# A hybrid SSD and HGRN2 trunk: dt block behind C, first convolution tap on ScalarE, states ahead of the taps, four output blocks begun together

## The reference

```python
h = rmsnorm(x, mix_norm[l])
z, xbc, dt_raw, q_raw, f_raw, i_raw, g_raw = split(h @ w_in[l])
xbc = silu(causal_depthwise_conv(xbc, conv_w, conv_b))      # 4 taps, B, C and xs
dt  = softplus(dt_raw + dt_bias);  a_cum = cumsum(dt * A)   # 8 heads
y_ssd = rmsnorm_groups((intra + inter + d * xs) * silu(z))  # SSD, state carried over chunks
f = lb + (1 - lb) * sigmoid(f_raw);  logf = log(f)          # HGRN2 gate
b = cumsum of logf over 16-token chunks
o = intra(q*exp(b-b_ref), k*exp(b_ref-b)) + inter(q*exp(b), state)
y_hg = rmsnorm_heads(o) * silu(g_raw)
x = x + concat(y_ssd, y_hg) @ w_out[l]
x = x + 0.5 * swiglu(rmsnorm(x))
```

## Time and profile before

| | us |
|---|---|
| median of three runs | 2044.61 (2044.28 to 2046.07) |
| profiled execution | 2046.51 |
| its span | 2044.7 |
| TensorE busy | 1989.8 (97% of the span) |
| VectorE busy | 801.9 (39%) |
| ScalarE busy | 661.9 (32%) |
| GpSimd busy | 845.4 (41%) |
| mean granted TensorE clock | 0.983 of full |

### The profile page before, as it was taken

The page is one execution under the profiler, slowest core; times in us unless marked ns, Lnnn a source line. Parts: engine busy times, 40 slices in busy tenths (PEclk is TensorE's granted clock), DMA queues, the critical chain, the costliest instruction groups (busy, mean ns, idle before and its releaser), DMA issues.

```text
span 2044.7 us, 29020 instructions
## 1 busy us (share of the span) xinstructions
PE 1989.8 (97%) x10636; PEld 1636.5 (80%) x10636; DVE 801.9 (39%) x1268; ACT 661.9 (32%) x903; POOL 845.4 (41%) x362
## 2 busy tenths in 40 slices
PE   7999999989989999999999999999799999999998
PEld 6888888867777888888888888888677778888887
DVE  7322211497786222221142222117778752222112
ACT  4323223343343322322232322224333332323222
POOL 3544444432223344444444444444322234444453
PEclk9999999989999999999999999999899899999999
DMA  3322333212112222233322223322211123223332
GB/s 136 122 92 94 97 94 95 93 63 69 58 52 87 85 96 97 98 94 94 101 94 94 100 94 95 96 89 82 73 64 52 43 92 101 94 92 100 96 94 91
DMA packets 55813, 181.62 MB, mean 89 GB/s; under 512 B 8369, under 2 KB 10417, under 8 KB 55729
## 3 DMA queue, kind: packets, MB, share of 16 engines
q1 hardware_dynamic: 55728, 180.52, 27.6%
HBM read 178.40 MB, written 2.10 MB: 88 GB/s over the span
## 4 chain that ended last, share of the span: by engine, by line
PE 84%; DVE 10%; issue 3%; ACT 1%; DMA 0%; DVEq 0%; SPq 0%; ACTq 0%
PE ps L1253 27%; PE ps L1254 27%; PE ps L1255 27%; DVE acc L865 1%; PE ps L1426 1%; DVE xs L904 1%; ACT th L510 1%; DVE b L872 1%; DVE lm L1058 1%; DVE g L852 0%; PE ps L1475 0%; DVE b L868 0%; PE ps L1268 0%; DVE e L939 0%; PE ps L1488 0%
## 5 line engine op out<-in xcount | busy, mean ns | idle before, releaser
L437 POOL TENSOR_TENSOR wlo<-raw,whi 128x1024 fp32r<-128x1024 f32 x348 | 843.1, 2424 | 1188.4 <-ACT whi L470 621.7
L1253 PE MATMUL ps<-hhi,whi 128*128 128x512 f32 x1776 | 703.0, 396 | 14.4 <-DVE w L967 13.7
L1254 PE MATMUL ps<-hlo,whi 128*128 128x512 f32 x1776 | 697.1, 393 | 0.0
L1255 PE MATMUL ps<-hhi,wlo 128*128 128x512 f32 x1776 | 696.6, 392 | 0.0
L1253 PEld LDWEIGHTS ps<-hhi,whi 128*128 128x128 f32 x1776 | 337.1, 190 | 91.3 <-issue 21.7
L1255 PEld LDWEIGHTS ps<-hhi,wlo 128*128 128x128 f32 x1776 | 337.0, 190 | 71.1
L1254 PEld LDWEIGHTS ps<-hlo,whi 128*128 128x128 f32 x1776 | 337.2, 190 | 68.6
L470 ACT ACTIVATE whi<-raw 128x1024 fp32r<-128x1024 f32 x168 | 177.2, 1056 | 344.6 <-PE ps L1255 344.6
L1255 PE MATMUL ps<-ahi,wlo 128*128 128x512 f32 x704 | 273.9, 389 | 0.0
L1253 PE MATMUL ps<-ahi,whi 128*128 128x512 f32 x704 | 273.9, 389 | 0.0
L1254 PE MATMUL ps<-alo,whi 128*128 128x512 f32 x704 | 273.9, 389 | 0.0
(11 more groups left out here) (228 smaller groups left out, 1466.1 us busy)
## 6 DMA issues: line engine op xcount, KB each, us to landing
raw<-in_up SPq DMA_DIRECT2D x168, 512.0 KB, 3.2
raw<-in_mix SPq DMA_DIRECT2D x66, 512.0 KB, 3.3
raw<-in_dn SPq DMA_DIRECT2D x64, 448.0 KB, 3.3
raw<-in_dn SPq DMA_DIRECT2D x32, 512.0 KB, 3.5
raw<-in_lead SPq DMA_DIRECT2D x12, 512.0 KB, 3.3
stage<-in_x SPq DMA_DIRECT2D x4, 512.0 KB, 7.0
out<-stage SPq DMA_DIRECT2D x8, 256.0 KB, 2.7
raw<-in_mix SPq DMA_DIRECT2D x4, 256.0 KB, 2.5
```

What stands on the lines that cost most here:

```text
L437: pool.tensor_tensor(wlo[:, q, :], raw[:, q, :], whi[:, q, :].bitcast(F32), ALU.subtract).then_inc(split.sem, 1)
L1253: mm(dst, whi[:, q, s], mh, start=start, stop=False)
L1254: mm(dst, whi[:, q, s], ml, start=False, stop=False)
L1255: return mm(dst, wlo[:, q, s], mh, start=False, stop=stop)
```

## The change

- `PROJ`: f3 and q0 move up and the dt block goes behind C; the value blocks follow q0 as before.
- The gate: `gate_f` is cut in two, the reciprocal goes straight into `b`, and the affine `b` operation on VectorE is replaced by scale and bias of ScalarE's Ln. Scans and the first distances stand before q0's bank is read; `hg_q(0)` and `query_levels(0)` come before `hg_dist(1)` and `hg_k(1)`.
- dt: `dt_first` behind C's work, `dt_rest` in the step of q3, `dt_turn` behind g0, `chunk_ends` behind xs0; TensorE waits for `dt_sum` and `b_tok` before the last k tile of g0.
- Convolution: the first tap, with its bias, is a ScalarE activation (`conv_start`); `hg_dist` stands ahead of the other taps of B and C, `ssd_states` ahead of those of xs1 to xs3.
- Output projection: blocks 0 to 3 each do their `SOON` tiles in four banks (4, 5, 0, 2), with `group_sums(1)` behind block 0's and `group_spreads(1)` behind block 2's, then their `LATE` tiles; the rest as before. On VectorE the last gates and norms change places.

The diff, without unchanged lines and step counts:

```diff
-PROJ = ([("f", 0), ("f", 1), ("f", 2), ("dt", 0), ("f", 3)]
-        + [("q", 0), ("q", 1), ("B", 0), ("q", 2), ("C", 0), ("q", 3), ("g", 0)]
+PROJ = ([("f", 0), ("f", 1), ("f", 2), ("f", 3), ("q", 0)]
+        + [("q", 1), ("B", 0), ("q", 2), ("C", 0), ("dt", 0), ("q", 3), ("g", 0)]
...
-VALUES_AFTER = 5
+VALUES_AFTER = 4
...
     if n < 0:
-        return VALUES_AFTER + k0 // 2
+        return VALUES_AFTER + 1 + k0 // 2
...
+        MIXED = (4, 5, 0, 2)
...
+                def conv_start(t, n):
+                    i = {"B": CONV_B, "C": CONV_C}.get(t, t)
+                    ready(proj_out, n)
+                    do(conv_first, conv_src(t), xr[:, 0:T], ACT.Identity,
+                       scale=par[:, CW + 4 * i:CW + 4 * i + 1], bias=par[:, CB + i:CB + i + 1])
...
+                def gate_log(p):
+                    ready(f_gate, p)
+                    do(f_log, b[:, p, :], b[:, p, :], ACT.Ln, scale=par[:, OLB + p:OLB + p + 1],
+                       bias=par[:, LB + p:LB + p + 1])
...
-                    if kind == "dt":
-                        ready(dt_abs)
-                        do(dt_exp, acb[:], acb[:], ACT.Exp)
...
                         for p in range(NP - 1):
-                            ready(f_gate, p)
-                            do(f_log, b[:, p, :], b[:, p, :], ACT.Ln)
-                        ready(dt_exp)
-                        do(dt_log, acb[:], acb[:], ACT.Ln, bias=1.0)
+                            gate_log(p)
                     if n == VALUES_AFTER:
-                        ready(f_gate, NP - 1)
-                        do(f_log, b[:, NP - 1, :], b[:, NP - 1, :], ACT.Ln)
+                        gate_log(NP - 1)
...
-                        hi(VALUES0 + 1 + NS)
-                        hg_exps(1)
...
-                        hi(VALUES0 + 2 + NS)
-                        hi(VALUES0 + 3 + NS)
+                        for i in range(1, VALUES):
+                            hi(VALUES0 + i + NS)
...
+                        hg_exps(1)
...
+                    if kind in ("B", "C"):
+                        conv_start(kind, n)
...
-                        ready(to_end)
-                        do(to_end_exp, wend[:], wend[:], ACT.Exp)
...
+                    if kind == "dt":
+                        ready(dt_abs)
+                        do(dt_exp, acb[:], acb[:], ACT.Exp)
+                        ready(dt_exp)
+                        do(dt_log, acb[:], acb[:], ACT.Ln, bias=1.0)
...
+                    if n == AT["z", 0]:
+                        ready(to_end)
+                        do(to_end_exp, wend[:], wend[:], ACT.Exp)
                     if kind == "xs":
+                        conv_start(pr, n)
...
+                            ssd_sq(3)
...
-                        if pr == 2:
-                            ssd_sq(3)
...
-                def gate_f(p):
+                def gate_first(p):
...
-                    did(dve.reciprocal(acc[:], t1[:]))
+                    did(dve.reciprocal(b[:, p, :], t1[:]))
+                def gate_last(p):
...
-                    did(stt(km[:, p, :], km[:, p, :], BIG, acc[:], ALU.min, ALU.mult))
-                    made(f_gate, ts(b[:, p, :], acc[:], col(OLB + p), col(LB + p), ALU.mult, ALU.add))
+                    made(f_gate, stt(km[:, p, :], km[:, p, :], BIG, b[:, p, :], ALU.min, ALU.mult))
...
-                def convolve(t, n):
+                def convolve(t):
...
-                    ready(proj_out, n)
-                    did(ts(dst, xr[:, 0:T], col(CW + 4 * i), col(CB + i), ALU.mult, ALU.add))
+                    ready(conv_first, CONVS.index(t))
                     for k in range(1, 4):
-                        settle()
+                        if k > 1:
+                            settle()
...
                 for n, (kind, pr) in enumerate(PROJ):
-                    evac(n)
-                    if n in (1, 2):
-                        gate_f(n - 1)
-                    if kind == "dt":
-                        dt_first()
-                        gate_f(2)
+                    if n != AT["q", 0]:
+                        evac(n)
+                    if kind == "f":
+                        if pr:
+                            gate_last(pr - 1)
+                        gate_first(pr)
                     if n == AT["f", 3]:
-                        gate_f(3)
-                        for p in range(NP - 1):
+                        gate_last(3)
+                    if n == AT["q", 0]:
+                        scan_f(0)
+                        hg_dist(0)
+                        for p in range(1, NP):
...
-                        hg_dist(0)
-                        scan_f(NP - 1)
-                        dt_rest()
+                        evac(n)
...
-                        hg_dist(1)
-                        did(dve.tensor_copy(acbs[0:8, :], acb[:]))
-                        settle()
-                        made(acb_split, tt(acbs[32:40, :], acb[:], acbs[0:8, :].bitcast(F32), ALU.subtract))
-                        hg_k(1)
-                    if n == AT["q", 0]:
...
+                        hg_dist(1)
+                        hg_k(1)
...
-                        if pr == 1:
-                            dt_out()
-                        if pr == 2:
-                            end_weights()
+                        if pr == 3:
+                            dt_rest()
...
+                        if pr == 3:
+                            ready(dt_sum)
+                            settle()
+                            did(dve.tensor_copy(acbs[0:8, :], acb[:]))
+                            settle()
+                            made(acb_split, tt(acbs[32:40, :], acb[:], acbs[0:8, :].bitcast(F32), ALU.subtract))
                     if kind in ("B", "C"):
-                        if kind == "B":
-                            ends()
-                        convolve(kind, n)
...
+                        convolve(kind)
...
+                    if kind == "dt":
+                        dt_first()
...
+                        dt_out()
...
-                        convolve(pr, n)
-                        conv_out(pr)
+                            ends()
...
+                        convolve(pr)
+                        conv_out(pr)
...
+                        else:
+                            end_weights()
...
-                    if kind == "g" and pr in (1, 2):
+                    if n == AT["g", 1]:
+                        ssd_states(3)
...
-                        silu(("g", pr), g2[:, 0, :], gs[:, pr % 2, :])
-                        if pr == 1:
-                            ssd_states(3)
-                        hg_gate(pr)
-                        if pr == 1:
-                            ssd_norm(0)
-                            ssd_norm(1)
-                            hg_norm(2, 3)
-                            hg_norm(3, 4)
-                            hg_lo(1)
-                        else:
-                            ssd_lo(0)
-                            ssd_lo(1)
-                            hg_lo(2)
-                            ssd_gate(3)
-                group_rsqrt(1)
+                        silu(("g", 1), g2[:, 0, :], gs[:, 1, :])
+                        hg_gate(1)
+                        ssd_norm(0)
+                        ssd_norm(1)
+                        hg_norm(2, 3)
+                        hg_norm(3, 4)
+                        hg_lo(1)
+                    if n == AT["g", 2]:
+                        ready(proj_out, n)
+                        silu(("g", 2), g2[:, 0, :], gs[:, 0, :])
+                        ssd_lo(0)
+                        ssd_lo(1)
+                        ssd_gate(3)
+                        hg_gate(2)
+                        hg_lo(2)
...
+                group_rsqrt(1)
+                hg_lo(3)
...
-                hg_lo(3)
...
-                        return stt(x[:, m, :], bank(DOWN + m % 2), 1.0, x[:, m, :], ALU.mult, ALU.add)
+                        return stt(x[:, m, :], bank(MIXED[m % 4]), 1.0, x[:, m, :], ALU.mult, ALU.add)
...
                 def b_turn():
-                    ready(to_end)
...
-                        ready(dt_sum)
...
-                        ready(b_tok)
+                        ready(to_end)
...
+                        if k == KD - 1 and n == AT["g", 0]:
+                            ready(b_tok)
+                            ready(dt_sum)
...
-                    if n == AT["q", 1]:
-                        dt_turn()
-                    if n == AT["B", 0]:
-                        chunk_ends()
...
                     if n == AT["g", 0]:
+                        dt_turn()
...
+                    if n == AT["xs", 0]:
+                        chunk_ends()
...
                                   else (ohi[:, k - NP, :], olo[k - NP][:]))
-                        last = products(bank(DOWN + m % 2), w % NS, k, moving, k == SOON[0], k == LATE[-1])
+                        last = products(bank(MIXED[m % 4]), w % NS, k, moving, k == SOON[0], k == LATE[-1])
...
```

(19 more changed lines are left out.)

## The result

The changed kernel takes 2024.98 us (median of four runs, 2022.80 to 2028.35) against 2044.44 us of the kernel before in the same rounds: ratio 0.9902, 95% interval 0.9881 to 0.9923. It is faster by 19.5 us; forecast were 40.8 us and 2004 us, with a range to 2021. The profiled execution took 2024.67 us, its span is 2022.9 us, the granted clock 0.990.

A forecast was written before the change was run, and what follows sets the result against it. TensorE, busy 97% of the span, was taken as the bound, with its idle and half-clock time to win. Gains 32.6 + 6.0 + 14.2 = 52.8 less new waits 12.0 gave net 40.8 us: 2044.61 to 2004 us, range 1990 to 2021.

The forecast's parts named there:

- Head of the mixer: End of the values to first HGRN2 outputs: `w` and `ks` waits with slow clock cost 16.3 us; 1.5 us remains.
- This wait goes: Head of the mixer: `ks` would be ready at 430.5 to 432.7 against TensorE's 432.6, so its wait disappears.
- B to g0: Mixer stretch that receives the moved dt chain: new waits of together 2.0 us per layer.
- The `dt_sum` term: At g0's last k, TensorE would newly wait 1.3 us for `dt_sum`, bounds 0 and 3.
- it is not on TensorE's path unless tanh of q3 is late, and that is hidden behind a GpSimd hold: Beside q3: two more ScalarE table switches per layer, 1.28 us each, would not delay TensorE.
- By the page's figure tanh of q3 would be 2.7 us later: At q3: with a switch costing 2.66 us, 2 us more over both layers, left out of the sum.
- SSD pairs: In the SSD pairs: states moved ahead of the taps remove four `st` waits, gaining 6.0 us.
- Output projection: Last projection matmul to FFN norm sums: `sqb` wait and slow clock, 7.1 us per layer, go; 2.5 new waits come.
- take VectorE some 2.8 each ... hidden: Output projection: four first residuals in a burst take VectorE 2.8 us each, hidden behind blocks 4 to 7 of 5.44.
- Waits of up to 1.8 us did not lower it: Argument against the upper-ends rival: TensorE waits of up to 1.8 us had not lowered the clock.
- waits at their upper ends: Rival for the whole mixer: new waits reach 20 us or more per layer, about 2018 to 2035; chance 0.20.
- The rival of GpSimd's hold: Rival, f0 to g0: 17 subtractions hold VectorE, which becomes the mixer's bound; slower, 2046 to 2055 us; chance 0.04.

The follow-up runs named there:

- e5: Changed kernel with GpSimd subtracting only 8 of 1024 columns per weight block after the first four, so VectorE is not held (result wrong): 1989.48 us.
- e6: Kernel before the change with GpSimd subtracting only 8 of 1024 columns per weight block after the first four (result wrong): 1990.6 us.
- e15: Changed kernel with e5's cut of GpSimd's subtraction and e1's order on ScalarE (result wrong): 1986.87 us.
- e1: Changed kernel with ScalarE's dt Exp and Ln placed behind the tanh of q3 instead of ahead of it: 2015.13 us.
- e12: Changed kernel with dt's Ln replaced by a second Exp, two table loads fewer per layer (result wrong): 2022.97 us.
- e7: Changed kernel with the dt block one place earlier, between q2 and C, and `dt_rest` in C's step: 2022.12 us.
- e2: Changed kernel with e1's order, and TensorE waiting for `dt_sum` only behind g0's outputs, right before the turn: 2020.74 us.
- e14: Changed kernel with the SSD states put back behind the convolution's taps: 2035.29 us.
- e8: Kernel before the change with only the output projection's part of the change: 2039.76 us.
- e13: Changed kernel with the first convolution tap and its bias back on VectorE: 2027.62 us.
- e11: Changed kernel with each GpSimd subtraction cut into four operations of 256 columns, plus e1's order: 2000.49 us, the fastest version that computes all.
- e3: Changed kernel with the 32 narrow head-sum matmuls cut in four groups of eight between xs1's k tiles: 2036.55 us.

## Why the prediction was wrong

The direction was right, and so were three of the four waits and the stages at both ends of the mixer taken whole; the size was half, 19.5 us of 40.8. By its own steps:

- **Head of the mixer, 16.3 less 1.5 us per layer.** 12.9 and 13.0 measured of 14.8. `w` comes 0.4 us late where 1.0 was taken. "This wait goes", said of `ks`, failed: 1.78 us remain. The working took off only operations and looked for no new hold; two of 0.18 us were held, 4.3 us together. e5, without holds, has no wait for `ks`. And the 16.3 us were not only "what both waits and their slow clock cost": in e6 both waits are gone, and B's block behind the scores and the eight dt transposes still takes 8.1 and 7.2 us, at a grant of 0.50 from 449 to 453, against 5.9 and 6.0 in e15, where the transposes stand behind g0. That part of the gain the sum had without knowing it; no run isolates the transposes as its cause.
- **B to g0, "together 2.0 us per layer".** This is the step that failed: 9.6 and 8.4 us were lost. The `dt_sum` term, 1.3 with bounds 0 and 3, is 4.7 and 4.3. Its error is one sentence: "it is not on TensorE's path unless tanh of q3 is late, and that is hidden behind a GpSimd hold". VectorE waited 5.00 us for tanh and ended the gate's step at 490.90; in e1, where tanh was in time and the same step was held to the full, it ended at 488.13. A hold covers what is late by less than itself, and this was more. e1 shows the order (9.9 us), e12 that the loads are about a third of the wait, e7 and e2 that neither a place further ahead nor a later wait frees VectorE. The remaining loss: -1.9 and -1.8 us up to outputs 1, with a wait for `hs` (1.3 us in the first layer) and more holds (`qs` at 452.05 took 2.73 us), and behind the `acb` wait half clock and the 0.8 us of moved work, together 2.4 and 1.7 us in the last row.
- **"By the page's figure tanh of q3 would be 2.7 us later".** In the trace the load is 1.28 us and the next activation starts 0.01 us behind it, in both places, so the drain that the Trainium skill gives (ScalarE: Activation LUTs, What ACT_TABLE_LOAD costs) does not show here. The rule of the same page of the Trainium skill that activations should be batched by table set (Table sets: the hidden batching unit) agrees in direction with e12, whose waits are 2.7 us shorter in sum with two loads fewer per layer; its time is not told apart from after. e1 keeps all loads and wins 9.9 us, so what cost most was not the loads but the critical tanh standing behind them.
- **SSD pairs, 6.0 us.** The `st` waits went, as said; e14 shows that this is worth 10 us and not 6. But the pairs show a gain of only 0.6 and 1.5 us per layer. "Had over 1 us to spare", said of the convolved x, failed: TensorE waits 1.3 us for `xde`, and the last pair takes 19.6 us in place of 17.9 (a rsqrt step of 0.2 us that VectorE does before it was held to 1.68 us; e5 has no such wait). In the first layer the clock took the rest: from the head sums to the first pair's output 10.9 us after and 10.1 before, 0.75 of which were a wait, against 9.3 in e1's first layer, where the clock did not fall. In the second layer the stretch is 12.5 us in both kernels, so there the fall is not new.
- **Output projection, 7.1 less 2.5 us per layer.** The two together were right, 4.6 forecast and 4.1 and 5.2 measured from the last pair's output to the norm sums, but by two errors that nearly cancel, which is luck. Up to the last out matmul 6.9 and 8.0 us were won, without the waits for `slo` and `olo`: `slo` ended at 598.5, 2.0 us ahead of the last projection matmul's end, where a wait of 1.2 us had been worked out. And "take VectorE some 2.8 each ... hidden" failed: 4.33 us each, 2.8 us per layer given back. It took the unheld lengths of operations that meet subtractions in each second residual. e8 gives back the same 2.8 us with this part alone.
- **"Waits of up to 1.8 us did not lower it"**, said of the clock: right for those; behind the narrow head sums it fell, now in both layers.
- **The rival "waits at their upper ends", 2018 to 2035,** is what happened, in size and partly in mechanism, at 0.20.
- **The rival of GpSimd's hold** had the right cause with the wrong sign and size: it asked whether the new order meets more holds than the old one. The holds did not make the change slower than before; without them nearly all waits for VectorE in the mixer go, in both kernels (e5, e6: 1989.5 and 1990.6 us), and a new order also chooses which operations meet them. (Its 17 subtractions from f0 to g0 are 16, which changes nothing.)

Taken away or done alone, the states' place is worth 10.3 us (e14), the projection about 7 (e8) and the first tap about 3 (e13), which is the 19.5 us already. The head's 26 us (12.9 and 13.0) are eaten to two thirds by the 18 us lost from B to the turn of xs0; the parts do not simply add, since one takes up slack that another leaves. Not tried: the head's reorder without the move of dt, and a subtraction tied to a free time of VectorE.

The holds fit what the Trainium skill describes (SBUF — State Buffer, Who interferes with whom): VectorE and GpSimd share one pair of ports as an exclusive lock for a whole instruction, and the one that comes second stands still. By that page this meets a VectorE instruction with two inputs in SBUF when GpSimd reads SBUF too, or one in a mode that uses both ports. The trace agrees on the length: 0.18 us operations end with 2.4 us subtractions, and quarter pieces cut the `acc` sum of the burst from 2.87 us (after) to 1.23 (e11), 0.69 unheld. That the port is the reason, and not something else that the two engines share, no run here isolates.

What of the clock stays open: when it falls behind the 32 head sums of 8 columns. The same stretch took 9.3, 10.9 or 12.5 us in different layers and kernels, also in e15 without any wait for another engine before it (12.5 in both layers). Of the 34 layers in the traces of all kernels but e3 it stayed up in five. By 3.2 us per layer that can be 6.4 us in an execution of the fastest version, an estimate (1.6 in its profiled one), and it scatters from run to run. e3, one profiled execution, points at the clump as the cause; it is no cure.

## What to carry to other kernels

Before forecasting a reorder, compare each operation's length with the same operation elsewhere (here 0.98 us became 2.11, and 0.18 became 2.43): the long ones are held, and a new order draws new lots for the holds. Remove such a cause (shorter GpSimd operations) before tuning the order by its symptoms. When a chain moves on one engine, follow what then stands ahead of the critical step on every other engine's queue: here an Exp and Ln ahead of one tanh cost 9.9 us, half as much as the whole change won.

## What the runs showed of the hardware

- GpSimd's subtraction takes 2420, 781 and 494 ns for 1024, 256 and 128 columns: about 0.21 us fixed and 2.2 ns per column. Pieces in quarters cost 24% more of GpSimd's time and save VectorE 31 us (e11).
- A hold did not depend on the size of the held operation: 16 columns took 2.43 us for 0.18, 512 columns 2.87 for 0.69, so both stood 2.2 us.
- 32 matmuls of 8 columns, with TensorE busy by the profile all the time, were followed by a grant of 0.62 and 0.52 in the changed kernel; with the sums spread between wide matmuls it was 1.00 (e3).
